# A gated recurrence whose decay levels are built by quarters in a ring of two instead of by halves

## The reference, cut to what matters

```
f = lb + (1 - lb) * sigmoid(z)          # z: own projection per direction
S_t = diag(f_t) S_(t-1) + (1 - f_t) v_t^T
o_t = S_t^T silu(q_t)                   # forward and backward outputs are added
```

## Time and profile before

| | |
|---|---|
| median of 3 runs | 2778.58 us (2778.49 to 2784.36) |
| the profiled execution's own time | 2778.75 us |
| its span, first to last instruction | 2777.1 us |
| TensorE busy | 2627.3 us (95%) |
| VectorE busy | 2032.8 us (73%) |
| ScalarE busy | 1456.1 us (52%) |
| GpSimd busy | 530.7 us (19%) |
| granted TensorE clock, mean | 0.977 of full |
| stretch 200 to 540 us: PE, DVE, ACT, POOL busy | 307.84, 222.91, 180.48, 161.99 of 340 us |
| granted clock there | 0.94 |

### The profile page before, as it was taken

One profiled execution on the slowest core, in us unless ns is written; L12 is line 12 of the kernel. 1 busy time (PEld: TensorE's weight loads), 2 busy tenths in 40 slices (PEclk: granted clock), 3 DMA queues, 4 the chain that ended last, 5 costly groups with the idle time before them and its releaser, 6 DMA issues. The chain is left out here.

```text
span 2777.1 us, 46798 instructions
## 1 busy us (share of the span) xinstructions
PE 2627.3 (95%) x16769; PEld 2252.4 (81%) x16770; DVE 2032.8 (73%) x2504; ACT 1456.1 (52%) x1644; POOL 530.7 (19%) x417
## 2 busy tenths in 40 slices
PE   7999988999897999999999999999999999999993
PEld 3897777778786789777887979899989897889793
DVE  5255776563765897999879787866686778977884
ACT  5255656212543664777657465544454546645653
POOL 0034554300023211122121111111121112111110
PEclk9999999999998999999999999999999999999997
DMA  7120111171343896999869787866586779967864
GB/s 292 48 70 24 42 41 56 60 260 58 110 103 114 328 381 222 369 357 353 316 232 362 254 302 269 284 205 208 192 304 204 254 237 333 331 211 280 298 230 136
DMA packets 274724, 605.97 MB, mean 218 GB/s; under 512 B 21868, under 2 KB 53012, under 8 KB 273520
## 3 DMA queue, kind: packets, MB, share of 16 engines
q1 hardware_dynamic: 254256, 561.62, 56.6%
q0 software_dynamic: 20384, 43.19, 7.0%
HBM read 582.09 MB, written 46.97 MB: 227 GB/s over the span
## 5 line engine op out<-in xcount | busy, mean ns | idle before, releaser
L2513 ACT ACTIVATE whi<-e_slot 128x2048 fp32r<-128x2048 f32 x296 | 560.9, 1912 | 393.2 <-PE e_acc L2430 326.9
L2575 DVE TENSOR_TENSOR e_slot_r<-e_slot,whi 128x2048 fp32r<-128x2048 f32 x296 | 674.9, 2287 | 106.4 <-ACT whi L2513 106.4
L2427 PE MATMUL e_acc<-e_xhi,whi 128*128 128x256 f32 x1664 | 398.7, 282 | 3.2 <-ACT e_xhi L2517 3.2
L2513 ACT ACTIVATE whi<-slot 128x2048 fp32r<-128x2048 f32 x148 | 283.3, 1914 | 192.1 <-PE e_acc L2402 192.1
L2575 DVE TENSOR_TENSOR slot_r<-slot,whi 128x2048 fp32r<-128x2048 f32 x151 | 344.8, 2286 | 18.1 <-ACT whi L2513 16.5
L2400 PE MATMUL e_acc<-whi,e_ahi 128*128 128x512 f32 x800 | 319.3, 399 | 0.0
L2427 PEld LDWEIGHTS e_acc<-e_xhi,whi 128*128 128x128 f32 x1664 | 313.1, 188 | 6.3 <-ACT e_xhi L2517 6.3
L2344 POOL DMA_INDIRECT sum<-yo,e_idx_now x50 | 120.6, 2412 | 1012.2 <-issue 539.2
L2402 PE MATMUL e_acc<-whi,e_alo 128*128 128x512 f32 x800 | 313.4, 392 | 0.0
L2401 PE MATMUL e_acc<-e_slot_r,e_ahi 128*128 128x512 f32 x800 | 311.6, 389 | 0.0
L2400 PE MATMUL e_acc<-whi,e_xhi 128*128 128x512 f32 x768 | 303.3, 395 | 0.4
(11 more groups left out here) (432 smaller groups left out, 5069.8 us busy)
## 6 DMA issues: line engine op xcount, KB each, us to landing
e_slot<-in_w SPq DMA_DIRECT2D x296, 1024.0 KB, 7.3
slot<-in_w SPq DMA_DIRECT2D x151, 1024.0 KB
rv<-in_w_ada SPq DMA_DIRECT2D x32, 512.0 KB, 5.2
slot<-in_w_in SPq DMA_DIRECT2D x9, 1024.0 KB, 9.8
wa<-in_w_ada SPq DMA_DIRECT2D x8, 1024.0 KB, 17.3
slot<-in_w_in SPq DMA_DIRECT2D x12, 512.0 KB, 4.7
xt<-in_x SPq DMA_DIRECT2D x8, 512.0 KB, 14.9
slot<-in_w_out SPq DMA_DIRECT2D x4, 1024.0 KB, 14.3
```

The costliest lines, as they stand in the source:

```text
L2427: pe.matmul(out[:, c, :], whi[i % RING][:, w], xhi[:, kk, :], start=first, stop=False, skip_group_check=True)
L2513: act.activation(whi[i % RING][:], raw[i % PIECES][:], ACT.Copy).then_inc(S["whi_made"], 1)
L2575: v.tensor_tensor(wlo[i % PIECES][:], raw[i % PIECES][:], whi[i % RING][:].bitcast(F32), ALU.subtract).then_inc(S["wlo_made"], 1)
```

## The change

- The unit is a quarter of two tiles (QT). `wk` and `wq` become one tile `wkq` and are used as a ring of two quarters: quarter c can be begun when the tiles of quarter c-2 are scored (`levels_free`). `lev_ready` counts quarters, `lev_sub` and `lev_exp` too.
- GpSimd makes the same four subtractions per level, each on 128 columns, twice as many.
- ScalarE takes keys and queries of a level from 1 on in one exponential over both.
- VectorE multiplies keys of both directions by one instruction for levels from 2 on (`key_of_blocks`; for it the keys of the two directions become neighbours in one tile).
- TensorE's list: scores 0, 1, 2, output 0, scores 3, output 1, a projection, outputs 2 and 3, three projections (five in head 0), the first query projection, scores 4, 5, 6, output 4, scores 7, output 5, the second query projection, outputs 6 and 7. The `keep_warm` calls in scores and outputs (20 or 4, 8 and 7 products) go, and in the transposes two calls of 10 become three of 8.
- VectorE's list: picks 2 and 3 move in between the levels of the third quarter, one weight remainder (`low_chunk`) moves ahead from behind the second cumulation, and the next head's second quarter is done behind both directions' states, before pick 0.
- ScalarE's copies, and GpSimd's roots, are placed anew among the quarters.

```
         wk_at = nc.sbuf_base
-        wk = t.sb("h_wk", [P, NL + 1, HN])
-        wq = t.sb("h_wq", [P, NL, HN])
+        wkq = t.sb("h_wkq", [P, 2 * NL + 1, HN])
+        wk, wq = wkq[:, 0:NL + 1], wkq[:, NL + 1:]
...
+        COPY_AT = [[4, 8, 10, 12, 13], [5, 7, 10, 13]]
...
+        def quarter(c):
+            return slice(c % 2 * QN, (c % 2 + 1) * QN)
+        def key_of_blocks(h, c, hl):
+            first = latent_key(h, 0, c // 2)[:, quarter(c)]
+            size = HN if c >= 2 else AN
+            return bass.AP(first.tensor, first.offset, [first.ap[0], (size + hl, 2), (2 * hl, QN // (2 * hl)), (1, hl)])
+        def levels_free(e, h, c):
+            if LT * h + QT * (c - 1) > 0:
+                e.wait_ge(S["s_done"], LT * h + QT * (c - 1))
...   TensorE
-                if i == 0:
-                    pe.wait_ge(S["lev_ready"], 2 * h + half + 1)
+                if j % QT == 0:
+                    pe.wait_ge(S["lev_ready"], 4 * h + j // QT + 1)
...
                 for j in range(HT):
                     scores(h, j)
-                    if j:
-                        if j == 1:
-                            keep_warm(ps[2], 4 if h else 20)
-                        output(h, j - 1)
+                    if j >= 2:
+                        output(h, j - 2)
...
-                output(h, HT - 1)
+                for j in range(HT - 2, HT):
+                    output(h, j)
...
+                    queries(h + 1, 0)
...
-                pe.wait_ge(S["picked"], 2 * (LT * h + 1))
-                keep_warm(ps[0], 8)
                 for j in range(HT, LT):
                     scores(h, j)
-                    if j > HT:
-                        if j == HT + 1:
-                            pe.wait_ge(S["picked"], 2 * (LT * h + 3))
-                            keep_warm(ps[2], 7)
-                        output(h, j - 1)
-                if more:
-                    queries(h + 1, 0)
-                output(h, LT - 1)
+                    if j >= HT + 2:
+                        output(h, j - 2)
                 if more:
                     queries(h + 1, 1)
+                for j in range(LT - 2, LT):
+                    output(h, j)
+                if more:
                     for n in range(6):
-                        if n in (2, 4):
+                        if n in (0, 2, 4):
                             pe.wait_ge(S["picked"], 2 * (LT * h + 7))
-                            keep_warm(ps[2], 10)
+                            keep_warm(ps[2], 8)
...   ScalarE
-                    act.wait_ge(S["lev_sub"], DIFF * h + half * DIFF // 2 + 4 * l)
-                    for x in (wk, wq):
-                        act.activation(x[:, l, :], x[:, l, :], ACT.Exp).then_inc(S["lev_exp"], 1)
+                    act.wait_ge(S["lev_sub"], DIFF * (4 * h + c) + 4 * l)
+                    x = wkq[:, l:2 * NL + 1:NL + 1, quarter(c)]
+                    act.activation(x, x, ACT.Exp).then_inc(S["lev_exp"], 1)
...
-                for l in range(NL):
-                    levels(h, 1, (l,))
-                    if l == 3:
+                for n in range(2 * NL):
+                    levels(h, 2 + n // NL, (n % NL,))
+                    if n == 7:
                         roots(h, 0)
+                    if more:
+                        if n in COPY_AT[h > 0]:
+                            copy_z(h + 1, COPY_AT[h > 0].index(n) + (2 if h else 0))
+                        if h and n == 11:
+                            high_chunk(3 * h + 5)
...
                     levels(h + 1, 0, range(3, NL))
+                    levels(h + 1, 1, range(NL))
                     gate_sig(h + 1)
...   GpSimd
-                    levels(h, 1, range(1, NL))
+                    levels(h, 2, range(1, NL))
+                    levels(h, 3, range(1, 2))
                     roots(h, 0)
+                    levels(h, 3, range(2, NL))
...
-                    levels(h + 1, 0, range(1, 3))
+                    levels(h + 1, 0, range(1, 5))
                     if h >= 0:
                         roots(h, 1)
-                    levels(h + 1, 0, range(3, NL))
+                    levels(h + 1, 0, range(5, NL))
+                    levels(h + 1, 1, range(1, NL))
                     gates(h + 1)
...   VectorE, in level
+                else:
+                    k4 = wk[:, l, at].rearrange("p (b f n) -> p f b n", f=2, n=hl)
+                    v.tensor_tensor(k4, k4, key_of_blocks(h, c, hl), ALU.mult).then_inc(S["lev_mul"], 1)
...
-                    pick(h, 2)
-                    pick(h, 3)
                     for l in range(NL):
-                        level(h, 1, l)
-                        if l == 4:
+                        level(h, 2, l)
+                        if l in (1, 3):
+                            pick(h, 2 + l // 2)
+                    for l in range(NL):
+                        level(h, 3, l)
+                        if l == 2:
                             finish(h, 0)
+                        if l == 5 and h and more:
+                            low_chunk(3 * h + 5)
...
-                    if now:
-                        low_chunk(3 * h + 5)
...
-                        if l == NL - 2:
-                            states(h + 1, 0)
+                    states(h + 1, 0)
                     states(h + 1, 1)
+                    for l in range(NL):
+                        level(h + 1, 1, l)
```

More of the change, by code:

```diff
@@ L387, in hgrn2 @@
         A_at = keep["rqk_at"] - 64
-        keyA = [at(f"h_keyA{d}", AN, A_at + 4 * AN * d, F32) for d in range(2)]
+        bothA = at("h_keyA", 2 * AN, A_at, F32)
+        keyA = [bothA[:, d * AN:(d + 1) * AN] for d in range(2)]
         cumA = at("h_cumA", AN, A_at + 8 * AN, F32)
@@ L391, in hgrn2 @@
         B_at = A_at + 12 * AN + 4 * (AN // P * STEP) + 8
-        keyB = [[at(f"h_keyB0{d}", HN, B_at + 4 * HN * d, F32) for d in range(2)]]
+        bothB = [at("h_keyB0", 2 * HN, B_at, F32)]
+        keyB = [[bothB[0][:, d * HN:(d + 1) * HN] for d in range(2)]]
         cumB = [at("h_cumB0", HN, B_at + 8 * HN, F32)]
@@ L949, in first_level @@
                     values_out(act)
-                fwd = latent_cum(h, half).rearrange("p (i f n) -> p i f n", f=2, n=HALF_TILE)
-                bwd = latent_ahead(h, half).rearrange("p i (f n) -> p i f n", f=2)
-                k4, q4 = view(wk[:, 0, :], HALF_TILE), view(wq[:, 0, :], HALF_TILE)
-                for i in range(HT):
-                    mf, mb = fwd[:, i, 0, HALF_TILE - 1:HALF_TILE], bwd[:, i, 1, 0:1]
+                fwd = cum_of(h, c).rearrange("p i (f n) -> p i f n", f=2)
@@ L955, in first_level @@
+                bwd = ahead_of(h, c).rearrange("p i (f n) -> p i f n", f=2)
+                k4, q4 = view(wk[:, 0, quarter(c)], HALF_TILE), view(wq[:, 0, quarter(c)], HALF_TILE)
+                for i in range(QT):
+                    mf, n = fwd[:, i, 0, HALF_TILE - 1:HALF_TILE], c * QT + i
                     act.activation(k4[:, i, 0], fwd[:, i, 0], ACT.Exp, scale=-1.0, bias=mf)
-                    k = act.activation(k4[:, i, 1], bwd[:, i, 1], ACT.Exp, bias=middle[:, h % 2, 1, half * HT + i:half * HT + i + 1])
+                    k = act.activation(k4[:, i, 1], bwd[:, i, 1], ACT.Exp, bias=middle[:, h % 2, 1, n:n + 1])
@@ L957, in first_level @@
                 k.then_inc(S["lev_exp"], 1)
-                for i in range(HT):
-                    mf, mb = fwd[:, i, 0, HALF_TILE - 1:HALF_TILE], bwd[:, i, 1, 0:1]
+                for i in range(QT):
+                    mb, n = bwd[:, i, 1, 0:1], c * QT + i
                     act.activation(q4[:, i, 0], bwd[:, i, 0], ACT.Exp, scale=-1.0, bias=mb)
-                    k = act.activation(q4[:, i, 1], fwd[:, i, 1], ACT.Exp, bias=middle[:, h % 2, 0, half * HT + i:half * HT + i + 1])
+                    k = act.activation(q4[:, i, 1], fwd[:, i, 1], ACT.Exp, bias=middle[:, h % 2, 0, n:n + 1])
@@ L1028, in _ @@
                     high_chunk(3 * h + 4)
-                    for i in range(2):
-                        copy_z(h + 1, i)
+                    if h:
+                        for i in range(2):
+                            copy_z(h + 1, i)
                 else:
@@ L1066, in _, with levels @@
         def _(g):
-            def levels(h, half, which):
-                g.wait_ge(S["s_done"], LT * h + half * HT)
-                if h == 0 and half == 0:
+            def levels(h, c, which):
+                levels_free(g, h, c)
+                if h == 0 and c < 2:
                     g.wait_ge(S["v_done"], NT)
```

88 lines of the change are left out of this document (48 added, 40 removed).

## The result

The changed kernel takes 2792.13 us (median of 6 runs, 2790.26 to 2797.7) where the kernel before takes 2778.85 in the same session (2778.39 to 2784.36): a ratio of 1.0045, 95% interval 1.0034 to 1.0055. I had forecast 2772.2. Its profiled execution took 2790.26 us, with a span of 2788.6.

What follows compares the result with a forecast made beforehand. Within the recurrence stage, TensorE and VectorE were taken to bound by turns. Head 0 +0.2, two cycles +0.2 each and the last leg −6.9 gave −6.3 us: 2772.2 us, range 2757 to 2785.

Steps and rivals of the forecast that it cites:

- slow-side rival: GpSimd's subtractions: fixed cost each, 128 columns as dear as 256, so held VectorE products pay 0.41 us; 2789.5, chance 0.16.
- Head 0: ... +0.2: First head: first pick still waits for its weight chunk, late query projection costs what earlier projections win; +0.2 us.
- mark P: Point where a head's last tile is picked and the next head's keys begin; 356.01 us in the kernel before.
- last leg: From the last head's mark to the stage's last output: +87.2 us against +94.1 before, a gain of 6.9 us.
- the cycle: Steady period from one head to the next in the recurrence: 88.9 us against 88.65, +0.2, counted twice.
- A to P: From a head's second quarter of levels ready (A) to its last pick and next keys (P): 46.6 us.
- P to A: From the next head's keys beginning to its second quarter of levels ready, VectorE's path: 42.3 us.
- gate product from about P+29: GpSimd's gate product, released after ScalarE's second-quarter exponentials, lasts 4.9 us and covers VectorE's second-quarter start up to P+34.
- slow blocks: TensorE's two scores and two outputs behind the tile 2 wait, at low clock: 8.0 us against 4.7.
- a held VectorE product: VectorE's level products beside GpSimd's 128-column subtractions, each held 0.21 us; all 17 of a quarter counted, 8.8 us each.
- Less holding, the first rival: GpSimd's subtractions finish before VectorE's levels, gate product falls beside the states: −6.7 us a cycle, twice; 2758.8, chance 0.24.
- second rival: TensorE's moved waits, in transposes and ahead of queries, bring another low-clock stretch, 3.3 us a cycle; 2778.8, chance 0.22.

Runs made afterwards that it cites:

- a_warm15: Changed kernel plus 15 warm-up products on TensorE, 8 and 7 in the waits ahead of tile 2's scores in heads 1 and 2; 2780.7 us, ratio 1.0008.
- the repeat: The changed kernel itself, unedited, run and profiled a second time beside later kernels; 2791.51 us, ratio 1.0047 to the kernel before.
- a_chunk_early: Changed kernel with ScalarE converting head 1's query weights (chunk 5) ahead of its last two key copies; 2787.90 us, ratio 1.0038.
- a_best1_split: The a_best1 kernel with the merged key product undone, two 128-column VectorE products for one of 256; 2777.76 us, ratio 0.9993.
- a_query_later: Changed kernel with head 0's first query projection put back behind the scores of tiles 4 to 7; 2793.17 us, ratio 1.0056.
- a_best1: Changed kernel plus 79 warm-up products, GpSimd's second quarter of head 0 behind VectorE's first, and chunk 5 converted early; 2769.17 us, ratio 0.9965.

## Why the prediction was wrong

- Failed, and by itself enough: "The change stays inside the gated-recurrence stage ..., so only that stretch can move." It changes the length of TensorE's program ahead of a loop, and that moved the loop by 316 instructions. It cost 10.0 us in the profile and, by a_warm15 against the changed kernel, 11 us in the runs. The slow-side rival that I gave (2789.5, a fixed cost on GpSimd) has nearly the right time for a wrong reason: 128-column subtractions are 0.39 us long alone.
- Failed, the step "Head 0: ... +0.2". It measured +8.4 at the mark P (+5.6 in the repeat). I wrote that a query projection that has to wait for its late weight remainder costs what the earlier ones win, and didn't work it out: chunk 5 is converted behind the last key copy, the projection waits 2.98 us and takes 7.2 (257.59 to 264.76) for 5.6, ahead of the scores of tile 4. a_chunk_early gives back 4.6 us of it by the marks, 3.2 against the repeat. The 3.4 us ahead of the first scores (2.0 in the repeat), GpSimd's queue against one long VectorE instruction, are in no step; I had charged GpSimd one instruction at a time.
- Right, the last leg: +87.2 from the mark, measured 87.8 (452.51 to 540.33; +94.1 before). Its gain is there; head 0's loss hides it. Two errors partly cancel in it: the scores of tile 2 came at +47.3 (499.78) for +45.5, and from them to the end were 40.6 us for 41.7.
- Right, the cycle: 88.9 predicted, 88.2 and 88.5 measured (90.9 and 88.6 in the repeat). A to P 46.6 against 45.0, since the slow blocks cost 6.3 us for 4.7 (319.03 to 325.33) and not 8.0, though the repeat has 8.2; P to A 42.3 against 43.2. In it: levels from P+15.2 (measured 15.3), first quarter at P+24.0 (26.0; VectorE stood 0.63 and 1.02 us for ScalarE's exponentials in it, a wait that the sum didn't have), states to P+30.8 (32.7), gate product from about P+29 (29.8).
- Right, and it was the largest unknown: a held VectorE product pays 0.2 us (I took 0.21). The merge I never priced by itself: my 1.9 us a head were for it and the halved tiles together, unheld, when beside GpSimd each instruction that it saves pays, 1.5 and 2.0 us a cycle by a_best1_split, and as much again and more by the clock behind the longer wait.
- Right: the waits of 9.2 and 9.0 us ahead of tile 2, the clock near 0.8 behind them, no wait ahead of the output of tile 5. Less holding, the first rival (2758.8), fell: the 48 subtractions queued from P on did hold. Of the second rival's low-clock stretches the one ahead of the queries was there in head 0 only (0.70 over 256 to 260 us). The one at the transposes was there before too, and is now a little deeper (0.70 and 0.50 over 372 to 380 us, for 0.82 and 0.75).
- Stage by stage: +8.4 for +0.2, -0.6 for +0.4 over two cycles, -6.3 for -6.9, then +10.0 for 0 (in the repeat +5.6, +2.3, -6.1 and +8.3). Without the last the change is worth +1.5 us here, which these measurements can't tell from nothing, and so the forecast of a gain fell too.

## What to carry to other kernels

An edit that changes how many instructions an engine has ahead of a large loop can cost or win several microseconds in the loop. Compare the waits for "issue" at the loop's head in both profiles before judging the edit, and pad or place the loop to make the comparison fair. When a wait is filled with a fixed number of products, look at it again after every edit: 0.8 to 1.5 us more of wait brought the low clock back, and that cost more than what had made the wait longer. Where VectorE and GpSimd work side by side, count VectorE's instructions and not only its columns, and keep long queues of small GpSimd instructions away from a VectorE instruction that TensorE waits for. When a reordering is summed up cycle by cycle, work out the first cycle as fully as the steady one: its offset is carried into all that follows, here in large part.

## What the runs showed of the hardware that was not expected

- From the stage's end to the end of the span are 2237 to 2243 us with one placement of the loop and 2247 to 2251 with another 60 instructions away (modulo 256). Its first product waits 2.5 to 2.9 or 8.7 to 10.2 us, and the second pass 3.3 to 3.6 us in the bad placement alone. Placed at the start of a line it waits 3.4 us, with 2239 us behind the stage.
- A 2048-column subtraction on VectorE waited for some twenty 128-column subtractions of GpSimd in a row (9.5 us for 2.5). The Trainium skill (SBUF — State Buffer, "two separate sides") has the shared port pair held for one instruction, and the other engine blocked for that long. In the levels this agrees (0.2 us a product); here it doesn't, VectorE got its turn only when GpSimd's queue was empty. That was so in four of seven profiles of kernels with the same code up to there, and 2.5 us in three; in one of these (a_query_later) it is GpSimd that stood, 3.8 us for two subtractions that otherwise take 0.8.
- TensorE's wait ahead of tile 2 costs more than its own length, and not the same each time: in two profiles of one kernel the blocks behind it took 6.3 and 8.2 us, where they take 4.9 at the full clock (a_best1).
